# A fused kernel for a two-layer transformer block and a hybrid block: how the heads of the latent attention are evicted and rotated

## The reference

```python
q = (rms_norm(cq) * mla_q_norm) @ mla_w_uq          # 384 -> 8 heads x 96
q = q.reshape(B, S, MLA_HEADS, MLA_NOPE + MLA_ROPE) # 64 plain + 32 rotated
q_nope = q[..., :MLA_NOPE].transpose(0, 2, 1, 3)
q_rope = rope(q[..., MLA_NOPE:], cos[:, None, :], sin[:, None, :]).transpose(0, 2, 1, 3)
ckv = rms_norm(ckv) * mla_kv_norm
k_nope = (ckv @ mla_w_uk).reshape(B, S, MLA_HEADS, MLA_NOPE).transpose(0, 2, 1, 3)
v = (ckv @ mla_w_uv).reshape(B, S, MLA_HEADS, MLA_V).transpose(0, 2, 1, 3)
k_rope = rope(kr, cos, sin)                         # one for all heads
...
s = (jnp.einsum('bhqd,bhkd->bhqk', qn, k_nope)
     + jnp.einsum('bhqd,bkd->bhqk', qr, k_rope)).astype(jnp.float32) * scale
```

## Time and profile before

| | |
|---|---|
| median of 3 runs | 3535.67 us (3535.11 to 3539.28) |
| the profiled execution: its own time | 3532.56 us |
| its span in the trace | 3530.8 us |
| PE busy | 3435.0 us (97%) |
| DVE busy | 1786.8 us (51%) |
| ACT busy | 1185.1 us (34%) |
| POOL busy | 287.3 us (8%) |
| mean granted PE clock | 0.983 of full |

### The profile page before, as it was taken

How to read it: one execution, slowest core, us unless ns; L and a number is a source line. 1 busy time by engine, 2 the same in 40 slices (tenths; PEclk the granted TensorE clock), 3 DMA queues, 4 the chain that set the end, 5 groups by cost and what they waited for, 6 DMA issues and landing times.

```text
span 3530.8 us, 40839 instructions
## 1 busy us (share of the span) xinstructions
PE 3435.0 (97%) x16646; PEld 2758.3 (78%) x16646; DVE 1786.8 (51%) x3100; ACT 1185.1 (34%) x1990; POOL 287.3 (8%) x238
## 2 busy tenths in 40 slices
PE   8999999999999999999899999999999999999999
PEld 6888786777888788887777878887788777878887
DVE  7666456565565733334654643334453655454433
ACT  3222236542222232223555332223321444223322
POOL 0000220002000200021200100013011000020000
PEclk9999999999999999999999999999999999999999
DMA  6565322123565523223210322322221223122232
GB/s 239 206 211 189 101 78 72 40 69 109 191 219 196 179 98 99 92 95 107 68 49 25 114 83 84 108 82 93 68 78 55 75 73 115 42 96 84 96 107 78
DMA packets 120218, 376.37 MB, mean 107 GB/s; under 512 B 13280, under 2 KB 28000, under 8 KB 120032
## 3 DMA queue, kind: packets, MB, share of 16 engines
q1 hardware_dynamic: 120032, 373.76, 31.8%
HBM read 371.61 MB, written 2.10 MB: 106 GB/s over the span
## 4 chain that ended last, share of the span: by engine, by line
PE 92%; DVE 4%; ACT 2%; issue 1%; POOL 1%; DMA 0%; SPq 0%; POOLq 0%; ACTq 0%; DVEq 0%
PE ps L445 26%; PE ps L446 26%; PE ps L447 26%; PE ps L660 2%; PE ps L683 2%; PE ps L554 2%; PE ps L488 1%; PE ps L495 1%; PE ps L479 1%; PE ps L481 1%; PE ps L480 1%; DVE s_wl L1429 1%; ACT s_wh L944 1%; POOL s_small L2109 0%; PE ps L521 0%
## 5 line engine op out<-in xcount | busy, mean ns | idle before, releaser
L445 PE MATMUL ps<-s_uh,s_wh 128*128 128x512 f32 x2824 | 1137.4, 403 | 30.2 <-DVE s_ul L1491 12.8
L1429 DVE TENSOR_TENSOR s_wl<-s_raw,s_wh 128x1024 fp32r<-128x1024 f32 (+3 forms) x645 | 707.1, 1097 | 845.2 <-ACT s_wh L944 843.0
L446 PE MATMUL ps<-s_uh,s_wl 128*128 128x512 f32 x2824 | 1111.1, 393 | 0.0
L447 PE MATMUL ps<-s_ul,s_wh 128*128 128x512 f32 x2824 | 1110.5, 393 | 0.0
L944 ACT ACTIVATE s_wh<-s_raw 128x1024 fp32r<-128x1024 f32 (+3 forms) x645 | 587.9, 913 | 727.6 <-PE ps L447 531.2
L445 PEld LDWEIGHTS ps<-s_uh,s_wh 128*128 128x128 f32 x2824 | 537.5, 190 | 173.1 <-issue 49.4
L447 PEld LDWEIGHTS ps<-s_ul,s_wh 128*128 128x128 f32 x2824 | 536.6, 190 | 115.1
L446 PEld LDWEIGHTS ps<-s_uh,s_wl 128*128 128x128 f32 x2824 | 537.9, 190 | 109.0 <-issue 2.4
L447 PE MATMUL ps<-s_fl,s_wh 128*128 128x512 f32 x960 | 378.2, 394 | 0.0
L445 PE MATMUL ps<-s_fh,s_wh 128*128 128x512 f32 x960 | 378.2, 394 | 0.0
L446 PE MATMUL ps<-s_fh,s_wl 128*128 128x512 f32 x960 | 378.2, 394 | 0.0
(11 more groups left out here) (401 smaller groups left out, 3374.1 us busy)
## 6 DMA issues: line engine op xcount, KB each, us to landing
s_raw<-w SPq DMA_DIRECT2D x616, 512.0 KB, 3.6
s_raw<-w SPq DMA_DIRECT2D x96, 192.0 KB, 2.4
s_raw<-w SPq DMA_DIRECT2D x64, 256.0 KB, 2.6
s_raw<-w SPq DMA_DIRECT2D x19, 128.0 KB, 2.0
s_x<-x SPq DMA_DIRECT2D x4, 512.0 KB, 6.3
out<-s_x SPq DMA_DIRECT2D x8, 256.0 KB, 2.2
s_raw<-w SPq DMA_DIRECT2D x4, 420.0 KB, 3.6
s_crow<-crow SPq DMA_DIRECT2D x2, 512.0 KB, 3.4
```

The source lines that it names most:

```text
L445: TE.matmul(o, w_hi(i, k), h, start=first, stop=False)
L446: TE.matmul(o, w_lo(i, k), h, start=False, stop=False)
L447: return TE.matmul(o, w_hi(i, k), l, start=False, stop=last)
L1429: V.tensor_tensor(wl[w][:, 0:n], raw[t % NRAW][:, 0:n], wh[w][:, 0:n].bitcast(F32), SUB).then_inc(*s_lo.up(("lo", t)))
```

## The change

DVE evicts a whole head with one multiplication of the full bank by a table of 128 rows: the score scale on rows 0 to 63 (new in the table), scale times cos on 64 to 95, scale times sin with its sign on 96 to 127. The two rotated products are no longer added. They stay as 64 separate rows of `mq`, and the keys' rotated part is written twice, on partitions 64 to 95 and 96 to 127, so that the sum over 128 rows in the score product adds them. ACT's eight copies of queries go, POOL's additions go, the seven key copies have 64 partitions instead of 32 and begin one head earlier. Scores contract over 128 rows. The DMA of the table is the same, in size and place.

```diff
--- before.py
+++ after.py
@@ -649,14 +649,13 @@
                         pe.wait_ge(*s_act["mk", st])
                         pe.wait_ge(*s_dve["mk", st])
                         pe.wait_ge(*s_dve["mq", st])
-                        pe.wait_ge(*s_pool["mq", st])
                         pe.wait_ge(*s_act["mv", st])
                     o = [take(("S", (st, 2 * t + g)), 2 * (t % 2 if kind == "mla" else 0) + g) for g in range(2)]
                     for g in range(2):
                         if kind == "nsa":
                             q, k = oA[64 * g:64 * g + 64, h, sl(i)], kk[64 * g:64 * g + 64, br, 0:L]
                         else:
-                            q, k = mq[0:96, 2 * h + g, sl(i)], mk[0:96, 2 * h + g, 0:L]
+                            q, k = mq[:, 2 * h + g, sl(i)], mk[:, 2 * h + g, 0:L]
                         TE.matmul(o[g][:, 0:L], q, k, start=True, stop=True).then_inc(*s_pe.up(("ps", ("S", (st, 2 * t + g)))))
                 for n in gate_pieces(t)[0:1]:
                     piece(*n)
@@ -1089,12 +1088,11 @@
                 copy(("pT", st, i), pcT[:, i, :, :].rearrange("p g n -> p (g n)"), bank(("pT", st, i))[:, 0:256], ("pcT", st))
             for h in range(8):
                 fm(f"uq{l}", 3, h)
-                copy(("uq", st, h), mq[0:64, h, :], bank(("uq", st, h))[0:64, :], ("mq", st, h), -(96.0 ** -0.5))
                 if h == 4:
                     apply(("ckv", st), 2, ch)
-                for h2 in {5: (1, 2), 6: (3, 4), 7: (5, 6, 7)}.get(h, ()):
+                for h2 in {4: (1,), 5: (2, 3), 6: (4, 5), 7: (6, 7)}.get(h, ()):
                     act.wait_ge(*s_dve["mk0", st])
-                    SC.activation(mk[64:96, h2, :], mk[64:96, 0, :], ACT.Copy).then_inc(*s_act.up(("mkr", st)))
+                    SC.activation(mk[64:128, h2, :], mk[64:128, 0, :], ACT.Copy).then_inc(*s_act.up(("mkr", st)))
             for i in range(4):
                 fm(f"uk{l}", 2, i)
                 copy(("uk", st, i), mk[0:64, 2 * i, :], bank(("uk", st, i))[0:64, :], ("mk", st))
@@ -1649,34 +1647,24 @@
             V.tensor_tensor(pv, pv, r.unsqueeze(2).broadcast_to([128, 32, 31]), MUL).then_inc(*s_dve.up(("pc", st, "scaled")))
             apply(("cq", st), ("cq", st), cq, 3, ("rq", st), qh, ql, lambda k: col(f"qn{l}", k))
             fm(f"inB{l}", 8, 5)
-            turns = [0]
-
-            def turn(dst, g, j, key, on_pool):
-                n = turns[0]
-                turns[0] += 1
-                t0, t1 = tmp[2 * (n % 2)], tmp[2 * (n % 2) + 1]
-                dve.wait_ge(*s_pe["ps", g])
-                dve.wait_ge(*table(f"rope {st}"))
-                if n > 1:
-                    dve.wait_ge(*s_pool["turned", st, n - 2])
-                if n == 6:
-                    dve.wait_ge(*s_dve["ckv", st, 1])
-                V.tensor_tensor(t0[64:96, :], bank(g)[64:96, :], rope[64:96, j, :], MUL).then_inc(*s_dve.up(("turn", st, n)))
-                V.tensor_tensor(t1[64:96, :], bank(g)[96:128, :], rope[96:128, j, :], MUL).then_inc(*s_dve.up(("turn", st, n), frees=g))
-                if not on_pool:
-                    dve.wait_ge(*s_dve.now())
-                    dve.wait_ge(*s_pe["ps", ("pT", st, 3)])
-                    V.tensor_tensor(dst, t0[64:96, :], t1[64:96, :], ADD).then_inc(*s_dve.up(key, ("added", st, n)))
-
             dve.wait_ge(*s_pool["rstd", ("ckv", st)])
             diag(("rk", st), acc, 36)
             for h in range(8):
                 fm(f"uq{l}", 3, h)
-                turn(mq[64:96, h, :], ("uq", st, h), 0, ("mq", st), h % 4 < 3)
+                g = ("uq", st, h)
+                dve.wait_ge(*table(f"rope {st}"))
+                dve.wait_ge(*s_pe["ps", g])
+                V.tensor_tensor(mq[:, h, :], bank(g)[:], rope[:, 0, :], MUL).then_inc(*s_dve.up(("mq", st), frees=g))
                 if h == 2:
-                    turn(mk[64:96, 0, :], ("dn", st, 5), 1, ("mk0", st), False)
+                    g = ("dn", st, 5)
+                    dve.wait_ge(*s_pe["ps", g])
+                    V.tensor_tensor(tmp[2][64:96, :], bank(g)[64:96, :], rope[64:96, 1, :], MUL).then_inc(*s_dve.up(("turned", st, 0)))
+                    V.tensor_tensor(tmp[3][64:96, :], bank(g)[96:128, :], rope[96:128, 1, :], MUL).then_inc(*s_dve.up(("turned", st), frees=g))
+                    dve.wait_ge(*s_pe["ps", ("pT", st, 3)])
+                    dve.wait_ge(*s_dve["turned", st])
+                    for r in (64, 96):
+                        V.tensor_tensor(mk[r:r + 32, 0, :], tmp[2][64:96, :], tmp[3][64:96, :], ADD).then_inc(*s_dve.up(("mk0", st)))
                 if h == 4:
-                    dve.wait_ge(*s_dve["added", st, 4])
                     apply(("ckv", st), ("ckv", st), ckv, 2, ("rk", st), ch, cl, lambda k: col(f"kvn{l}", k))
             for i in range(4):
                 fm(f"uk{l}", 2, i)
@@ -1704,8 +1692,6 @@
                         dve.wait_ge(*s_pe["ps", ("S", (st, n))])
                         if n > 5:
                             dve.wait_ge(*s_pe["ps", ("T", (st, n - 6))])
-                        else:
-                            dve.wait_ge(*s_pool["turned", st, 7])
                         V.tensor_tensor_reduce(mP[n % 6][:, 0:L], bank(("S", (st, n)))[:, 0:L], bias, 1.0, 3.0e38, ADD, MIN, two(n, 0)).then_inc(
                             *s_dve.up(("s", (st, n)), *([("slope used", st, h)] if kind == "nsa" else []), frees=("S", (st, n))))
                 if t > 0:
@@ -2155,22 +2141,9 @@
             for g in range(2):
                 for i in range(4):
                     PO.tensor_copy(p5v[:, i, g, :, :], pc.rearrange("p (i h g n) -> p i h g n", i=4, h=4, g=2)[:, i, :, g, :]).then_inc(*s_pool.up(("p5", st)))
-            n = 0
-            pool.wait_ge(*s_pe["ps", ("pT", st, 3)])
-            for h in range(8):
-                t0, t1 = tmp[2 * (n % 2)], tmp[2 * (n % 2) + 1]
-                if h % 4 < 3:
-                    pool.wait_ge(*s_dve["turn", st, n])
-                    PO.tensor_tensor(mq[64:96, h, :], t0[64:96, :], t1[64:96, :], ADD).then_inc(*s_pool.up(("turned", st, n), ("mq", st)))
-                else:
-                    s_pool.mark(("turned", st, n))
-                n += 1
-                if h == 2:
-                    s_pool.mark(("turned", st, n))
-                    n += 1
             pool.wait_ge(*table(f"dist {st}"))
             pool.wait_ge(*s_pe["latent", st])
-            pool.wait_ge(*s_dve["added", st, 8])
+            pool.wait_ge(*s_dve["mk0", st])
             pool.wait_ge(*s_pool.now())
             for h in range(4):
                 for g in range(2):
@@ -2344,6 +2317,7 @@
     ang = np.arange(512, dtype=f)[:, None] * inv[None, :].astype(f)
     co, si = np.cos(ang.astype(np.float64)).T.astype(f), np.sin(ang.astype(np.float64)).T.astype(f)
     rope = np.zeros((128, 2, 512), f)
+    rope[0:64, 0] = f(-(96.0 ** -0.5))
     for i, sc in enumerate((f(-(96.0 ** -0.5)), f(1))):
         rope[64:96, i] = sc * np.concatenate([co, co])
         rope[96:128, i] = sc * np.concatenate([-si, si])
```

## The result

| | before | after |
|---|---|---|
| median | 3535.64 us (3532.71 to 3540.25, 8 runs) | 3528.16 us (3523.33 to 3533.98, 8 runs) |
| after / before | | 0.9968 [0.9957, 0.9979] |
| profiled execution, its span | 3532.56 us, 3530.8 us | 3529.91 us, 3528.0 us |

The ratio stands for 11.3 us (0.0032 x 3535.6; interval 7.4 to 15.2), the two medians are 7.5 us apart, and 9.25 us had been forecast. The two profiled spans are only 2.8 us apart. The stage of the change, and what lies outside it, tell why that is too little.

What follows compares the result with a forecast made beforehand. PE, busy 97% of the span, bounds the kernel, so only its stalls count. First layer 3.74, second 3.91, clock 1.6: 9.25 us off the median 3535.67 gives 3526.4 us, range 3522.5 to 3531.5.

Steps and rivals of the forecast that it cites:

- Step 1: Ahead of the row of scales, the keys' bank is free 0.72 us earlier in each layer; 2.23 us of stall stay.
- Step 2: Head 7's weights come earlier, net of one ACT key copy: 0.69 and 0.86 us; about 0.6 us of stall stay.
- Step 3: From head 7's start to the values' start, 10.43 us becomes 8.1: 2.33 us saved in each layer.
- the collision: Second key product's low-part subtraction takes 1.57 instead of 0.42 us, starting with a POOL addition of 1.30 us.
- the late third product: Third key product stalls 0.90 us: its low part comes late after the slow subtraction, behind head 7's three-operation turn.
- the second rival: ACT's key copies or the values' weights come late, so head-7-to-values gains nothing: 3532.7 us, chance 0.17.
- Step 4: From the values to the first scores 6.61 us unchanged; scores over 128 rows cost nothing more, bounds -2.6 to +20 us.
- the slower rival: Scores over 128 rows cost 157 ns more per record, a loss of 20 us: 3546.5 us, chance 0.03.
- Step 5: Clock drop behind the stall at the row of scales: one of two drops goes, 1.6 us, bounds 0 and 3.2.
- the first rival: The clock stays up in both layers behind the shortened stall: 3524.8 us, chance 0.15.
- The wait that changes hands: Same as the second rival: late key copies or values' weights leave only 3.0 us gained, 3532.7 us, chance 0.17.
- The stall blamed on ACT: Rival: second key product's 1.32 us stall comes from ACT's key copies and remains in both layers: 3529.0 us, chance 0.05.

Runs made afterwards that it cites:

- runs 2 and 4: Kernel before without POOL's query additions: stage 38.79 / 38.77 us; kernel before with head 6's POOL addition held until the colliding low part is done: 3535.97 us.
- run 6: Changed kernel with ACT's copy of query rows 0 to 63 back and DVE multiplying rows 64 to 127 only: 3526.81 us, stage 35.21 / 36.80 us.
- run 3: Kernel before with ACT's seven key copies made at heads 3 and 4 instead of 5 to 7: 3537.53 us, stage 39.62 / 39.63 us.
- run 9: Changed kernel with ACT's key copies back at heads 5, 6 and 7 only: 3521.68 us, stage 33.48 / 35.07 us.
- run 5: Changed kernel with three POOL additions for heads 4 to 6 put back, writing to unread scratch: 3521.64 us, stage 34.00 / 34.00 us.

## Why the prediction was right, step by step

The total of 9.25 us lies inside what the ratio allows (7.4 to 15.2), and the stages give about 10.6 us (below): the mechanism held and two terms were too small. That the median lands within 2 us of the forecast is also luck, since the two comparisons of the same two kernels gave 7.5 and 7.0 us between their medians, and 11.3 and 9.2 us by their ratios.

**Step 1, 0.72 us.** Measured 0.74 and 0.73, and the stall that stays is 2.23 us to the digit. Right.

**Step 2, 0.69 and 0.86 us.** Measured 0.88 and 1.03, and 0.43 us of the stall stay instead of 0.6. The parts, first layer: from head 4's eviction to the latent 1.98 us became 0.61, a gain of 1.37 where I had 1.26. From the latent to the rounding of head 7's weights 1.98 us (524.22 to 526.20) became 2.74 (522.12 to 524.86): the key copy costs 0.76 with what stands around it, not 0.57. From the rounding to PE 1.43 us became 1.17: I had left out that DVE was itself late there in before. 1.37 - 0.76 + 0.26 is 0.87. Right in kind, 0.17 to 0.19 us too small. ACT's rows of after:

```profile
524.21 0.63 ACT L1095 ACTIVATE s_mk<-s_mk 64x512 f32<-64x512 f32 x1
524.86 0.53 ACT L943 ACTIVATE s_wh<-s_raw 128x384 fp32r<-128x384 f32 x1
```

**Step 3, 2.33 us.** Measured 2.35 and 2.36; the values start 8.08 us behind head 7. The size was right because it was worked out from PE's own pace and the chain to the values' weights, and not from the stalls that went. The links of that chain in after, ACT and DVE:

```profile
531.66 1.05 ACT L943 ACTIVATE s_wh<-s_raw 128x1024 fp32r<-128x1024 f32 x1
```

```profile
532.74 1.23 DVE L1427 TENSOR_TENSOR s_wl<-s_raw,s_wh 128x1024 fp32r<-128x1024 f32 x1 [0.38 <-ACT s_wh L943]
```

The second key product ends 5.10 us behind head 7's start (the prediction had 5.06), and 0.53, 1.08, 1.23 and 0.14 us follow to the values. The prediction's own terms add up to 8.03, which it wrote as 8.1. The cause that it led with, the collision, is real and is 0.93 us of it (10.43 to 9.50, runs 2 and 4). The other 1.42 us are the operations that DVE and ACT no longer make. Of these ACT's copies are 1.09 when they are put back into after (run 6); that the last 0.3 are DVE's is what remains, and no run shows it. The step took the two low parts as one story; the late third product was not an effect of the collision, since its 0.9 us stayed when that went. The margins were about half of what the step gave: in after the low parts of the second, third and fourth key product end 0.51, 0.27 and 0.59 us before PE starts on them, not 1.0, 0.8 and 1.2. They still covered ACT's key copies, but the second rival was nearer than its chance of 0.17 was argued from.

**Step 4, nothing.** 6.61 us unchanged, 612 ns for 512 columns in 96 and in 128 rows. Right, and the slower rival fell with it.

**Step 5, 1.6 us for one fall of two.** The size of a fall was right (1.57). Its chance was the weak step. The stall of 2.95 us was followed by a fall in 10 of 10 cases (five traces of the kernel before and its variants, two layers each), that of 2.23 us in 2 of 10 (five traces of after and its variants). By these counts the change saves 2 x (39.61 - 34.0 - 0.2 x 1.57) = 10.6 us, 1.3 more than forecast; the measured ratios, 0.9968 and 0.9974, are 11.3 and 9.2 us. Neither "one of two falls" nor the first rival's "never" is right as a rule: each profile is a draw. The Trainium skill ("TensorE: Matmul & The Clock Gate", section "Why this matters for your kernels") warns of idle gaps longer than this one only; the two falls behind 2.23 us, one behind the 2.11 us of run 6 and two behind the 2.15 us of run 3 show that shorter gaps can do it.

**The rivals.** The wait that changes hands came, small: 0.23 us ahead of the values, and run 9 shows that the moved copies cause it together with head 7's 0.43. The stall blamed on ACT went. What the prediction called scatter of 2 us in the runs is larger: over 11 runs the changed kernel spread over 14.7 us. Its range was said to take in most of the second rival, but ended at 3531.5 us, below that rival's 3532.7.

## What to carry to other kernels

When one engine bounds the kernel, cost an edit by that engine's pace to its next fixed point, not by adding up the stalls that the edit seems to remove. Where a short operation of DVE takes several times its usual time, look at what POOL started in the same tenth of a microsecond; moving one of them is enough, and so is slack that is longer than what the loser loses. And measure a stage by its own start and end when the run-to-run scatter of the whole program is as large as the effect.

## What the runs showed of the chip

- A race that is decided by hundredths of a microsecond. The 128x256 subtraction takes 0.42 us if it starts first, be it by 0.01 us (run 5), and 1.54 to 1.57 us if POOL's addition does, or starts with it. In the kernels with the order of before, the addition takes 1.52 to 1.56 us behind such a subtraction and 1.26 to 1.32 us where it does not have to wait. DVE's multiplications with one operand from a bank showed no such stretching: in before they took 0.69 or 0.70 us beside every addition of POOL, and in run 5 the one at 527.43 took 0.68 beside an addition that ran from 527.10 for 1.32 us.
- The clock does not follow from the length of a stall alone: 1.30 to 1.47 us brought a fall in none of 12 cases, 2.11 us in 1 of 2, 2.15 us in 2 of 2, 2.23 us in 2 of 10, 2.95 us in 10 of 10. What decides between them stays open; a difference in what PE did before the stall was not tried.
- Half clock for 27 us without a stall of PE (the same 31 matmuls in 9.62 against 5.50 us), in one of two profiled executions of the same kernel. Its cause is open too. In each of the 14 traces the clock was at half for 113 to 140 us in all.
- The cost of a DVE eviction from a bank does not depend on its rows (32, 64 and 128: 0.69 us), nor that of ACT's key copies on 32 and 64 (two take 1.15 us in both kernels), nor a float32 matmul's between 96 and 128 (612 ns).
